# Reordering the end of each state-space group: spread B/C rows, output transposes and the decode norm row

## The reference, cut to what matters

```python
xbc = silu(causal_dwconv(xbc) + ssm_conv_b)            # x: 256 columns, B: 128, C: 128 per group
dt = softplus(dt_raw + ssm_dt_bias)
y_b, S = ssd_chunked(xs_, dt, A, Bm, Cm, S0)           # chunks: (C B' * decay) x, and the carried state
y_b = (y_b + D * xs_) * silu(z)
y_b = rmsnorm(y_b.reshape(.., GROUPS, 256), norm_w)    # per group and token
```

## Time and profile before

| | us |
|---|---|
| median of three runs | 3505.74 |
| the profiled execution | 3503.55 |
| its span, first to last instruction | 3501.80 |
| TensorE busy | 3342.1 (95%) |
| VectorE busy | 1696.7 (48%) |
| ScalarE busy | 1024.4 (29%) |
| GpSimd busy | 967.9 (28%) |

### The profile page before, as it was taken

How to read it: one execution, slowest core, us unless ns; L and a number is a source line. 1 busy time by engine, 2 the same in 40 slices (tenths; PEclk the granted TensorE clock), 3 DMA queues, 4 the chain that set the end, 5 groups by cost and what they waited for, 6 DMA issues and landing times.

```text
span 3501.8 us, 55140 instructions
## 1 busy us (share of the span) xinstructions
PE 3342.1 (95%) x21375; PEld 3191.1 (91%) x21375; DVE 1696.7 (48%) x2656; ACT 1024.4 (29%) x2240; POOL 967.9 (28%) x438
## 2 busy tenths in 40 slices
PE   8899999999999999999999899999899999999998
PEld 7899999998899999899999778999658999999998
DVE  5766566666300367878777833141342242323133
ACT  5344334344311244443444522031231110101010
POOL 3221122222121221111111102224324444444452
PEclk9999999999999999999999999999889999999999
DMA  4111101111222223322322354223121111111111
GB/s 134 50 45 44 43 24 49 43 49 38 94 83 78 85 67 81 86 75 73 92 84 80 96 191 165 64 97 102 60 103 42 49 42 48 42 48 48 47 43 67
DMA packets 339221, 249.59 MB, mean 71 GB/s; under 512 B 13652, under 2 KB 320413, under 8 KB 339029
## 3 DMA queue, kind: packets, MB, share of 16 engines
q1 hardware_dynamic: 323310, 228.32, 21.7%
q10 hardware_dynamic: 15792, 19.60, 1.6%
HBM read 201.57 MB, written 46.78 MB: 71 GB/s over the span
## 4 chain that ended last, share of the span: by engine, by line
PE 75%; DVE 14%; issue 4%; ACT 4%; DMA 1%; POOL 1%; DVEq 0%; ACTq 0%; SPq 0%; POOLq 0%
PE psum L1490 9%; PE psum L1492 9%; PE psum L1491 9%; PE psum L1034 8%; PE psum L1036 8%; PE psum L1035 8%; PE psum L1168 4%; PE psum L1344 2%; PE psum L1346 2%; PE psum L1345 2%; DVE arena L2229 2%; PE psum L1159 1%; PE psum L1552 1%; PE psum L1304 1%; PE psum L1526 1%
## 5 line engine op out<-in xcount | busy, mean ns | idle before, releaser
L1034 PE MATMUL psum<-xh,whe 128*128 128x344 f32 x2304 | 776.9, 337 | 0.5 <-issue 0.5
L1035 PE MATMUL psum<-xl,whe 128*128 128x344 f32 x2304 | 743.3, 323 | 0.0
L1036 PE MATMUL psum<-xh,wle 128*128 128x344 f32 x2304 | 743.2, 323 | 0.0
L3039 POOL TENSOR_TENSOR wle<-slab,whe 128x1024 fp32r<-128x1024 f32 x104 | 256.8, 2470 | 1449.7 <-ACT whe L1641 1449.7
L1034 PEld LDWEIGHTS psum<-xh,whe 128*128 128x128 f32 x2304 | 441.3, 192 | 4.6 <-issue 2.5
L1035 PEld LDWEIGHTS psum<-xl,whe 128*128 128x128 f32 x2304 | 441.6, 192 | 0.6
L1036 PEld LDWEIGHTS psum<-xh,wle 128*128 128x128 f32 x2304 | 439.2, 191 | 0.0
L3131 POOL TENSOR_SCALAR wparts<-slab 128x1024 fp32r<-128x1024 f32 x80 | 221.9, 2774 | 500.0 <-POOLq L68 500.0
L1490 PE MATMUL psum<-at,wparts 128*128 128x344 f32 x960 | 309.7, 323 | 4.0 <-DVE r L2948 4.0
L1492 PE MATMUL psum<-at,wparts 128*128 128x344 f32 x960 | 308.2, 321 | 0.0
L1491 PE MATMUL psum<-xlow,wparts 128*128 128x344 f32 x960 | 306.2, 319 | 0.0
(11 more groups left out here) (420 smaller groups left out, 6579.9 us busy)
## 6 DMA issues: line engine op xcount, KB each, us to landing
slab<-in_w_in_dram SPq DMA_DIRECT2D x96, 512.0 KB, 3.9
arena<-d_rows SPq DMA_DIRECT2D x40, 512.0 KB, 5.6
slab<-in_w_ff_up_dram SPq DMA_DIRECT2D x32, 512.0 KB, 3.9
slab<-in_w_ff_down_dram SPq DMA_DIRECT2D x32, 512.0 KB, 3.7
out_dram<-arena SPq DMA_DIRECT2D x24, 512.0 KB, 4.5
arena<-in_state_ssm_dram SPq DMA_DIRECT2D x16, 512.0 KB, 6.2
d_yb<-arena SPq DMA_DIRECT2D x16, 512.0 KB, 4.5
slab<-in_w_ssm_up_dram SPq DMA_DIRECT2D x16, 512.0 KB, 3.7
```

The costliest lines, as they stand in the source:

```text
L1034: pe.matmul(out, w_hi, a_hi, start=(k == 0), stop=False)
L1035: pe.matmul(out, w_hi, a_lo, start=False, stop=False)
L1036: mm = pe.matmul(out, w_lo, a_hi, start=False, stop=(k == KT - 1))
L3039: pool.tensor_tensor(rounded(wle[slot]), slab[slot][:, :], whe[slot], ALU.subtract).then_inc(wlo_ready, 1)
```

## The change

It works on the end of each group.

- **PE.** With a group to fill for, the decode rows `bb` and `cc` are no longer one block behind `fs`: the four products go in behind chunk 7, each followed by 4 units, in place of `fill("scan7")` and `fill("fs")`; then `fs`. The 16 units of `norm` are split: 8 ahead of `to0`, then 2 behind each of `to0` to `to3`. `n8` moves behind `to3`. In the last group, which has keys and values of the memory as filler, only `n8` moves.
- **Banks.** `rw`, `n8`, `fs` are tied to bank 7, `bb`, `cc`, `to` to banks 3 to 6; `tb` to `cb` shift accordingly.
- **ACT.** The square root comes ahead of emptying the parts of `scan7` and `fs`, and both are emptied ahead of the final state's move. The parts of `norm` come behind the eight scalings, and the `n8` square root behind these. The tanh of tile 3 (`stanh(g+1, 3)`) moves from the end of the group into the next group's body, behind `decays(g, 0)` (in the last group behind `tb`).
- **DVE.** Behind chunk 7 stands nothing of the convolution. The reciprocal of the norm comes between the `bb` and the `cc` half of the decode step. `mix2` goes ahead of `to0`; the `n8` result follows `to3`; the four taps of tile 3 come last, behind `yb_ready`; `mix3` moves to the start of the next group's body, behind `shx`.

```diff
-        snames = ["rw"] + ["tb0", "tb1", "tx0", "tx1", "tx2", "tx3", "t8", "cb0", "cb1"]
+        snames = [("rw", 7)] + ["tb0", "tb1", "tx0", "tx1", "tx2", "tx3", "t8", "cb0", "cb1"]
...
-        snames += [("fs", 7), "bb0", "bb1", "cc0", "cc1", "n8", "to0", "to1", "to2", "to3"]
+        snames += [("fs", 7)] + [(f"{n}{j}", 3 + 2 * i + j) for i, n in enumerate(("bb", "cc")) for j in range(2)] \
+            + [("n8", 7)] + [(f"to{p}", 3 + p) for p in range(4)]
...
                 pe.wait_ge(bc8_ready, g + 1)
...
                 if more:
-                    fill("norm")
-                pe.wait_ge(y8sq_ready, g + 1)
-                hand(G, "n8", g, lambda bk: (
...
+                    first = sfills(f"scan{NC - 1}")[0]
+                    for i in range(4):
+                        spread_rows(i // 2, i % 2)
+                        bcxz(g + 1, first + 4 * i, first + 4 * i + 4)
+                    final_state()
...
+                a, z = sfills("norm")
+                if more:
+                    bcxz(g + 1, a, z - 8)
+                else:
                     fill("norm")
                 for p in range(4):
                     pe.wait_ge(ys_ready, NC * g + 2 * p + 2)
                     hand(G, f"to{p}", g, lambda bk, p=p: (
...
+                    if more:
+                        bcxz(g + 1, z - 8 + 2 * p, z - 6 + 2 * p)
+                pe.wait_ge(y8sq_ready, g + 1)
+                hand(G, "n8", g, lambda bk: (
...
                 act.wait_ge(shs_ready, g + 1)
                 decays(g, 0)
+                if more and not first:
+                    stanh(g, 3)
                 evac("tb")
                 if more:
                     high_weights((6 * g, W_SSM + 7))
...
+                act.wait_ge(ysq_ready, NC * g + NC)
+                act.activation(ssq, ssq, ACT.Sqrt, scale=1.0 / (2 * P), bias=eps[:, :]).then_inc(yroot_ready, 1)
+                evac(f"scan{NC - 1}")
+                if more:
+                    evac("fs")
                 act.wait_ge(srw_stored, 96 * g + 96)
                 move(G, "fs", g, stf, lambda bk: bk[:, 0:2 * P])
...
                 if then:
                     high_weights((6 * g, W_SSM + 12))
-                if more:
-                    stanh(g + 1, 3)
...
                 act.wait_ge(yrn_ready, g + 1)
                 for c in range(NC):
                     part_ = yt[:, 2 * P * c:2 * P * (c + 1)]
                     act.activation(part_, part_, ACT.Copy, scale=srn[:, c:c + 1]).then_inc(ys_ready, 1)
+                evac("decode")
                 evac("norm")
+                move(G, "n8", g, r8[:, 0:NB], lambda bk: bk[:, 0:NB], ACT.Sqrt, scale=1.0 / (2 * P), bias=eps[:, :])
...
-                        "scan6": [(2, 3)], "scan7": [(3, 0), (3, 1), (3, 2), (3, 3), "mix2"], "end": ["mix3"]}
+                        "scan6": [(2, 3)], "norm": ["mix2"], "end": [(3, 0), (3, 1), (3, 2), (3, 3)]}
...
                 dve.tensor_copy(shx, dtx[:, bass.ds(g * 34, 34)]).then_inc(shx_ready, 1)
+                if not first:
+                    mix(g, 3)
                 if more:
                     conv_columns(g + 1)
...
                 for p in range(4):
                     taken(G, f"to{p}", g)
                 dve.sem_inc(yb_ready, 1)
+                beside("end")
```

More of the change, by code:

```diff
@@ L1417, in body, with spread_rows @@
-                fill("decode")
-                if more:
-                    fill("norm")
-                pe.wait_ge(y8sq_ready, g + 1)
-                hand(G, "n8", g, lambda bk: (
-                    pe.matmul(bk[:, 0:NB], ones[:, :], sq8[:, q * NB:(q + 1) * NB], start=(q == 0), stop=(q == 1))
-                    for q in range(2)))
-                if not more:
+                    if c < NC - 1:
+                        fill(f"scan{c}")
+                def spread_rows(part_, j):
+                    hand(G, f"{('bb', 'cc')[part_]}{j}", g, lambda bk: (
+                        pe.matmul(cols(bk, i), ident[0:NB, 4 * j + i:4 * j + i + 1].broadcast_to([NB, P]),
+                                  bc8[:, part_ * P:(part_ + 1) * P], start=True, stop=True) for i in range(4)))
@@ new lines, in final_state @@
+                def final_state():
+                    taken(G, "su7", g)
+                    hand(G, "fs", g, lambda bk: (
+                        pe.transpose(bk[:, i * P:(i + 1) * P], cols(SST[0], i), ident[:, :]) for i in range(2)))
+                pe.wait_ge(bc8_ready, g + 1)
+                if more:
+                    first = sfills(f"scan{NC - 1}")[0]
[4 more added lines that the diff above has]
+                else:
+                    fill(f"scan{NC - 1}")
+                    final_state()
+                    fill("fs")
+                    for i in range(4):
+                        spread_rows(i // 2, i % 2)
+                    fill("decode")
@@ L1430, in body @@
                         for i in range(4)))
+                    if more:
+                        bcxz(g + 1, z - 8 + 2 * p, z - 6 + 2 * p)
+                pe.wait_ge(y8sq_ready, g + 1)
+                hand(G, "n8", g, lambda bk: (
+                    pe.matmul(bk[:, 0:NB], ones[:, :], sq8[:, q * NB:(q + 1) * NB], start=(q == 0), stop=(q == 1))
+                    for q in range(2)))
             body(0, True)
@@ L2039, in body @@
                                   ).then_inc(stf_stored, 16)
[L2040 removed]
+                if not more:
+                    evac("fs")
                 if then:
                     high_weights((6 * g, W_SSM + 12))
[L2043 to L2048 removed]
                 act.wait_ge(yrn_ready, g + 1)
@@ L2725, in body @@
                 dve.tensor_tensor(sq8, y8, y8, ALU.mult).then_inc(y8sq_ready, 1)
-                dve.wait_ge(yroot_ready, g + 1)
-                dve.reciprocal(srn, ssq).then_inc(yrn_ready, 1)
-                beside("end")
-                taken(G, "n8", g)
-                do(dve.reciprocal(r8[:, NB:2 * NB], r8[:, 0:NB]))
-                dve.wait_ge(ysq_ready, NC * g + NC)
-                for q in range(2):
-                    dve.scalar_tensor_tensor(out=yo8[q], in0=y8[:, q * NB:(q + 1) * NB], scalar=snw[:, q:q + 1],
-                                             in1=r8[:, NB:2 * NB], op0=ALU.mult, op1=ALU.mult)
+                beside("norm")
                 for p in range(4):
@@ L2740, in body @@
                     give(G, f"to{p}", ins)
+                taken(G, "n8", g)
+                do(dve.reciprocal(r8[:, NB:2 * NB], r8[:, 0:NB]))
+                dve.wait_ge(ysq_ready, NC * g + NC)
+                for q in range(2):
+                    ins = dve.scalar_tensor_tensor(out=yo8[q], in0=y8[:, q * NB:(q + 1) * NB], scalar=snw[:, q:q + 1],
+                                                   in1=r8[:, NB:2 * NB], op0=ALU.mult, op1=ALU.mult)
+                do(ins)
                 for p in range(4):
```

31 lines of the change are left out of this document (11 added, 20 removed).

## The result

The kernel after takes 3527.66 us (median of four runs, 3525.39 to 3529.84) against 3505.82 of the kernel before beside it: a ratio of 1.0061, 95% interval 1.0043 to 1.0078. It is 22 us slower, outside the forecast's range of 3480 to 3513. Its profiled execution took 3527.24 us, with a span of 3525.5; that is 23.7 us more than the one before.

A forecast was written before the change was run, and what follows sets the result against it. PE, busy 95% of the span, bounds the kernel. Tails -47, heads +23, their clock +7 and the last group +6 give -11 us against 3503.55, 3492.6; with 2.2 for the median, 3494.8, range 3480 to 3513.

The forecast's parts named there:

- Tails, -47: Seven tails: waits and slow clock worth 54.8 us go, new waits and cuts add 8.0, so 47 us gained.
- cover of about zero: Tail: PE wants `to0` at +16.7 us, just after ACT's first two scalings at +16.6.
- 0.44: Tail's end: PE waits 0.44 us between `n8` and the next group's `rw` in the same bank, seven times.
- I take that it does: Tails: spreading the rows keeps the clock up, so all clock loss goes; 14 us less gain if only half.
- Heads, +23: Six heads: the chain put into DVE's slack makes each 23.1 us in place of 19.24, 23 us lost.
- upper bound of 33: Six heads: most they could lose, 6 x 5.5 us, if POOL's tile slows `mix4` and `mix5` as well.
- Clock at `cb0`, +7: Heads: the clock falls behind a wait of some 3 us in four of six, 7 us lost, between 0 and 20.
- Last group, +6: Last group's head: the reciprocal ACT waits for comes at R+14.3 instead of R+8.3, 6 us lost, between 3 and 7.
- The slower one: Rival: clock falls at `cb0` in six heads and around `n8` and `rw` in seven tails, 3519.7 us; chance 0.11.
- spreading the rows would not keep the clock up: Rival: the tails' long clock falls stay, 18.8 us, giving 3513.6 us; chance 0.08.
- `shs` well before R+7: Sign in the head: forecast wrong if DVE's `shs` comes much before R+7, counted from the next group's `rw`.

The follow-up runs named there:

- rows apart: Kernel after, with four dense units ahead of each block of spread rows instead of behind it: 3519.34 us, ratio 1.0038.
- experiment 2: Kernel after, with DVE's column copies moved behind the z part and ACT's weight tile behind `decays(g, 2)`: 3495.22 us, ratio 0.9972.
- experiment 3: Kernel after, with `mix3` moved behind `xdt` and `xdd` on DVE, the tanh staying late: 3470.56 us, ratio 0.9904.
- experiment 8: Kernel after, tile 3's tanh ahead of `decays(g, 0)`, dense units ahead of each spread-row block, last group's memory-row reciprocal ahead of the third `tx` part: 3456.68 us.
- Experiment 9: Kernel after, with tile 3's tanh ahead of `decays(g, 0)` and the four spread-row blocks in one piece behind all 16 units: 3481.47 us.
- experiments 1: Kernel after, with tile 3's tanh on ACT moved ahead of `decays(g, 0)` and its wait for `shs`: 3466.87 us, ratio 0.9889.
- experiment 5: Kernel after, with tile 3's four taps back behind chunk 7, and its tanh and `mix3` back at the group's end: 3469.55 us, ratio 0.989.

## Why the prediction was wrong, point by point

The forecast had the places right and the head's size wrong.

**Tails, -47: measured -37.7.** The hand-overs went as told: no wait before `to0` (the cover of about zero held), none before `n8`, 0.36 us before `rw` where 0.44 was taken. What failed is "I take that it does": the clock stayed up only in the first tail, and its fall cost 1.7 us in each of the other six, 10 us. With rows apart the tails give -47.4: the term was sized rightly for a kernel that keeps its clock, and the premise that spread rows keep it up was wrong for blocks that begin right behind the wait. The long falls of the earlier trace rows did go.

**Heads, +23: measured +41.5.** This is the step that failed, and it was outside its own upper bound of 33. Point by point, R = 1560.06: `shs` copied at R+6.4 (I had R+7.3: the return of the loop, 1.06 us in the earlier trace rows, is hidden behind the taps), tanh R+10.0 to R+11.0 (R+11.9), `mix3` done at R+12.3 (R+13.1). So far the chain was 0.8 us faster than told. Then the column copies, 0.7 in my sum, took till R+14.9, where R+14.0 was forecast; and from `tx` to `cb0` it took 11.3 us, not 9.1, with `mix4` and `mix5` at 4.54 in place of 2.38. R+26.2 against R+23.1 is -1.1 for the chain, 2.0 for the collision at the copies and 2.2 for that at `mix5`. PE stood ready at R+19.2, near the R+18.7 told, so the wait before `cb0` was 7.0 us and not 3. I had put the second collision into the bound alone, at 1.6 us a head, and had taken POOL's first tile as something that only PE might wait for. The trace of the kernel before has rows for both, of POOL in the head of the earlier trace rows and of DVE ahead of the tail:

```profile
1781.34 2.41 POOL L3039 TENSOR_TENSOR wle<-slab,whe 128x1024 fp32r<-128x1024 f32 x1 [28.34 <-ACT whe L1641]
...
1732.66 3.52 DVE L2229 SCALAR_TENSOR_TENSOR arena<-arena,tables 128x1024 f32<-128x1024 f32 x1
```

The tile starts at R+11.7 there. With the 1.6 us by which I had it delayed it starts at R+13.3, in the midst of my own place for the copies, R+13.1 to R+14.0. And L2229, of 1.28 us alone, took 3.52 beside a tile of POOL that began at 1732.69: 2.2 us more, the size of the second collision, was on record too.

**Clock at `cb0`, +7: measured +12.8**, in the middles. The fall came in six of six, where I took four, and PE had 4.6 us at the lower clock behind it, 2.3 to 2.5 us lost each, where I took 3.3 us and 1.7 lost. The longer wait goes with that: behind 7.0 us it fell always, behind 3.1 in part (experiment 2), behind 1.0 never (experiment 3).

**Last group, +6: measured +5.3** in its head, +5.6 in the wait. Right, and half of it can be had back (experiment 8).

**The sum** with measured terms, -37.7 + 41.5 + 12.8 + 5.3, is +21.9 in place of -11: 9 us from the tails' clock, 18.5 from the head, 6 from the clock at `cb0`, less 1 from the last group.

**Rivals.** The slower one (clock falls in the new places, 3519.7) was nearest, in part by luck: right that the clock falls at every `cb0`, though 2.4 us lost each and not 3.3, wrong around `n8` and `rw`, where no fall was seen, and without the collisions that made the time. That spreading the rows would not keep the clock up was half right: the first block's place decided it.

**What makes the clock fall.** The Trainium skill's rule (TensorE: Matmul & The Clock Gate, section HAM oscillation) blames idle gaps of PE, longer ones than the 0.9 to 1.0 us of the tails here. The fall at `cb0` agrees, since it began while PE stood. Experiment 9 does not: there the clock fell while PE had been busy for 12 us. No rule for small matmuls comes out of these runs either. The block in one piece brought a fall in seven of seven tails there, but in `before` the one of the earlier trace rows ran at 1.00. And with the first block right behind the wait, the same PE instructions in the same order brought a fall in six tails (after), three (experiments 1 and 2), two (experiment 3) and four (experiment 5) of seven. What the runs do show is that dense work between the wait and blocks of 1.15 us ended the falls. What sets the clock off stays open.

**What would show it wrong** was named as `shs` well before R+7. It came at R+6.4, and the time was lost behind it all the same: that sign was a poor one.

## What to carry to other kernels

When work is moved into an engine's slack, lay out the other engines' order behind the move as well: what an engine waits for, ahead of its critical work, should be issued first by the engine that makes it, and a GpSimd tile that slides onto VectorE's SBUF-to-SBUF instructions holds up the critical engine: by 2.0 and 2.2 us a group here. Look for such instructions, longer than their like, in the trace before the change. One statement ahead of or behind nine others decided between -1.1% and +0.6% here. Put dense matmuls between a wait and a run of small ones.

## What the runs showed of the hardware that was not expected

- A VectorE copy of 128x29 took 2.18 us beside a GpSimd tile of 2.40 us, and 0.18 without. Of two SBUF-to-SBUF instructions of 1.2 us each, the second took 3.39; the GpSimd tile that began under the first took 3.30 in place of 2.40. Beside instructions that read PSUM (4.88 us for eight, both ways) there was no such cost. That a copy of 29 columns waits for the rest of a whole tile was the surprise, though the trace of before has such a case (L2231, 8 columns, 2.36 us in place of 0.22, at 1312.96).
- The clock fell to its lower level with TensorE busy throughout, for 3.4 us, in the last 0.3 us of a block of 3.90 us of matmuls with 8 contraction rows that stood behind dense work. The four blocks apart, 1.15 us each between dense stretches of 1.9 us, left it at 1.00 in all of 28 tails of four kernels. Where the first block stood right behind 0.86 to 1.03 us of idle time and the small matmuls of chunk 7, it fell in 18 of 35 tails of five kernels (after and experiments 1, 2, 3 and 5), for 1.7 or 5.1 us lost.
- At `cb0` the fall went with the length of the idle time ahead of it: behind 7.0 us the clock fell in six heads of six, behind 3.1 in three, behind 1.0 in none.
